# Low pieces of x on GpSimd, and the router's product with its matrix stationary

## The reference, cut to what matters

```python
scores = jax.nn.sigmoid((x @ router_w).astype(jnp.float32))          # 256 x 64
grouped = (scores + router_b).reshape(t, N_GROUPS, N_EXPERTS // N_GROUPS)
group_score = jnp.sum(lax.top_k(grouped, 2)[0], -1)
_, top_groups = lax.top_k(group_score, TOPK_GROUPS)
...
_, idx = lax.top_k(masked, TOP_K)
gate = jnp.take_along_axis(scores, idx, -1)
gate = gate / jnp.sum(gate, -1, keepdims=True) * ROUTED_SCALE
```

## Time and profile before

| | us |
|---|---|
| median of 3 runs | 1355.67 (1354.36 to 1355.84) |
| the profiled execution | 1355.5 |
| its span | 1353.8 |
| PE busy | 1306.0 (96%) |
| DVE busy | 419.1 (31%) |
| ACT busy | 309.5 (23%) |
| POOL busy | 28.2 (2%) |

### The profile page before, as it was taken

The page is one execution under the profiler, slowest core; times in us unless marked ns, Lnnn a source line. Parts: engine busy times, 40 slices in busy tenths (PEclk is TensorE's granted clock), DMA queues, the critical chain, the costliest instruction groups (busy, mean ns, idle before and its releaser), DMA issues.

```text
span 1353.8 us, 16202 instructions
## 1 busy us (share of the span) xinstructions
PE 1306.0 (96%) x6237; PEld 655.2 (48%) x6237; DVE 419.1 (31%) x899; ACT 309.5 (23%) x671; POOL 28.2 (2%) x101
## 2 busy tenths in 40 slices
PE   7999999999999999999979999999999999999996
PEld 5877854344343434444336555444434343443432
DVE  3667364112121121212133655421212212121213
ACT  4354331112111211111121343112111211111112
POOL 1003000000000000000000000000000000000000
PEclk9999989999999999999999998999999999999998
DMA  9315056899999999999992618399999999999992
GB/s 340 127 44 215 1 240 257 324 375 418 418 418 416 417 419 418 417 417 419 418 350 81 248 62 347 150 357 374 418 418 418 416 418 418 418 417 418 418 417 102
DMA packets 93653, 446.27 MB, mean 330 GB/s; under 512 B 9975, under 2 KB 12458, under 8 KB 60330
## 3 DMA queue, kind: packets, MB, share of 16 engines
q1 hardware_dynamic: 93222, 445.51, 81.7%
q10 hardware_dynamic: 388, 0.17, 0.1%
HBM read 444.60 MB, written 1.05 MB: 329 GB/s over the span
## 4 chain that ended last, share of the span: by engine, by line
PE 81%; DMA 12%; DVE 3%; ACT 1%; SPq 1%; issue 1%; DVEq 0%
PE psum L411 28%; PE psum L473 12%; DMA w_up_ring<-in_moe_w_up 12%; PE psum L424 9%; PE psum L465 7%; PE psum L1975 4%; PE psum L2117 4%; PE psum L1095 3%; PE psum L569 2%; PE psum L1538 2%; PE psum L1384 1%; PE psum L1134 1%; PE psum L450 1%; PE psum L602 1%; SPq L294 1%
## 5 line engine op out<-in xcount | busy, mean ns | idle before, releaser
L411 PE MATMUL psum<-w_up_ring,moe_x_selected 128*64 128x512 f32 x2048 | 450.8, 593 | 8.0 <-DMA w_up_ring<-in_moe_w_up 8.0
L411 PEld LDWEIGHTS psum<-w_up_ring,moe_x_selected 128*64 128x64 f32 x2048 | 146.2, 137 | 302.0 <-issue 284.9
L473 PE MATMUL psum<-w_down_ring,moe_hT 128*64 128x512 f32 x992 | 226.5, 598 | 0.9 <-ACT moe_hT L765 0.9
L967 DVE SCALAR_TENSOR_TENSOR moe_h<-moe_silu,moe_slot_gate,psum 128x256 f32<-128x256 f32 x64 | 30.7, 480 | 386.6 <-ACT moe_silu L758 386.6
L473 PEld LDWEIGHTS psum<-w_down_ring,moe_hT 128*64 128x64 f32 x992 | 65.7, 136 | 129.7 <-issue 128.3
L758 ACT ACTIVATE moe_silu<-psum 128x256 f32<-128x256 f32 x64 | 24.7, 385 | 415.2 <-PE psum L411 415.2
L985 DVE TENSOR_TENSOR moe_out_low<-psum,moe_out_high 128x512 fp32r<-128x512 f32 x64 | 44.3, 692 | 233.6 <-ACT moe_out_high L770 233.6
L465 PE MATMUL psum<-moe_out_high,moe_matchT 128*128 128x512 f32 x256 | 113.8, 444 | 0.0
L424 PE MATMUL psum<-moe_match,moe_x_high 128*128 128x448 f32 x256 | 102.4, 400 | 0.0
L465 PE MATMUL psum<-moe_out_low,moe_matchT 128*128 128x512 f32 x256 | 101.4, 396 | 0.0
L424 PE MATMUL psum<-moe_match,moe_x_low 128*128 128x448 f32 x256 | 93.3, 364 | 0.0
(11 more groups left out here) (498 smaller groups left out, 1120.8 us busy)
## 6 DMA issues: line engine op xcount, KB each, us to landing
w_up_ring<-in_moe_w_gate SPq DMA_DIRECT2D x128, 1024.0 KB, 13.1
w_up_ring<-in_moe_w_up SPq DMA_DIRECT2D x128, 1024.0 KB, 15.3
w_down_ring<-in_moe_w_down SPq DMA_DIRECT2D x124, 1024.0 KB, 14.8
w_up_ring<-in_ev_w_in SPq DMA_DIRECT2D x4, 2048.0 KB, 14.2
w_up_ring<-in_od_w_in SPq DMA_DIRECT2D x4, 2048.0 KB, 15.4
w_up_ring<-in_ev_w_out SPq DMA_DIRECT2D x2, 2048.0 KB, 7.8
moe_w_down_extra<-in_moe_w_down SPq DMA_DIRECT2D x4, 1024.0 KB, 16.5
w_up_ring<-in_od_w_out SPq DMA_DIRECT2D x2, 2048.0 KB, 7.7
```

The lines of the kernel that those rows point to most:

```text
L411: last = nc.tensor.matmul(k.psum[e * SLOTS:(e + 1) * SLOTS, 6, :], xsel[:, kk, own:own + SLOTS], up_view(slots[e], kk), start=kk == 0, sto ...
L473: last = nc.tensor.matmul(k.psum[e * SLOTS:(e + 1) * SLOTS, bank, :], hT[:, j * P + e * SLOTS:j * P + (e + 1) * SLOTS], places[e][:, j, ha ...
```

## The change

In each layer: `x_low` is subtracted by POOL, ahead of its memset, and no longer by DVE. The router's product has the router's 128x64 matrix as the stationary operand and 128 tokens as the moving one, so its result is 64 experts by 128 tokens; the sigmoid works on that and writes it to `scores_turned`, and PE turns it back by a transpose into PSUM, which raises `scores`. DVE adds the bias from PSUM, and copies the scores to SBUF with one more operation. ACT takes `scores(0)` ahead of `high_part(0)` and `scores(1)` ahead of `high_part(1)`. On PE, `turn_scores(0)` stands between `turn_x(1)` and `logits(1)`, and `turn_scores(1)` behind the first chunk of `shared_up(0)`.

```diff
+    scoreT = at("scores_turned", [N_EXP, NT, P], F32, end)
...
-                last = nc.tensor.matmul(k.psum[:, 3 * t, 0:N_EXP], k.xT[:, kk, t * P:(t + 1) * P], k.router_w[:, kk, :],
+                last = nc.tensor.matmul(k.psum[0:N_EXP, 3 * t, 0:P], k.router_w[:, kk, :], k.xT[:, kk, t * P:(t + 1) * P],
                                         start=kk == 0, stop=kk == KD - 1)
             last.then_inc(s.logits, 1)
+
+        def turn_scores(t):
+            pe.wait_ge(s.sigmoid, t + 1)
+            nc.tensor.transpose(k.psum[:, 3 * t, P:P + N_EXP], scoreT[:, t, :], k.ident[0:N_EXP, 0:N_EXP]).then_inc(s.scores, 1)
...
         turn_x(1)
+        turn_scores(0)
         logits(1)
         pe.wait_ge(s.shared_w, 32)
-        shared_up(0, range(5))
+        shared_up(0, range(1))
+        turn_scores(1)
+        shared_up(0, range(1, 5))
         pe.wait_ge(s.selected, 1)
...
         def scores(t):
             act.wait_ge(s.logits, t + 1)
-            nc.scalar.activation(score[:, t, :], k.psum[:, 3 * t, 0:N_EXP], ACT.Sigmoid).then_inc(s.scores, 1)
+            nc.scalar.activation(scoreT[:, t, :], k.psum[0:N_EXP, 3 * t, 0:P], ACT.Sigmoid).then_inc(s.sigmoid, 1)
...
         nc.scalar.activation(w1.early[:], w1.ln_eps[:], ACT.Sigmoid)
+        scores(0)
         high_part(0)
         take_xT(1)
-        scores(0)
+        scores(1)
         high_part(1)
-        scores(1)
...
+        for t in range(NT):
+            pool.wait_ge(s.x_high, t + 1)
+            nc.gpsimd.tensor_tensor(x_low[:, t], k.x[:, t, :].rearrange("p (c k) -> p k c", k=KD), x_high[:, t],
+                                    ALU.subtract).then_inc(s.parts, 1)
         pool.wait_ge(s.normed1, NT)
...
         def group_heads(t):
             dve.wait_ge(s.scores, t + 1)
-            step(nc.vector.tensor_tensor(biased[:, t, :], score[:, t, :], k.router_b[:], ALU.add))
+            turned = k.psum[:, 3 * t, P:P + N_EXP]
+            step(nc.vector.tensor_tensor(biased[:, t, :], turned, k.router_b[:], ALU.add))
+            step(nc.vector.tensor_copy(score[:, t, :], turned))
...
         dve.wait_ge(x.router, 32)
-        low_part(0)
         group_heads(0)
-        low_part(1)
         group_heads(1)
```

More of the change, by code:

```diff
@@ L282 @@
     experts="router gu0 gu1 dn0 dn1 dn_extra",
-    moe="mixed variance1 root1 normed1 tables shared_w shared_wd xT_psum xT dve x_high parts logits scores selected places "
+    moe="mixed variance1 root1 normed1 tables shared_w shared_wd xT_psum xT dve x_high parts logits sigmoid scores selected places "
             "table_sb table_dram "
```

## The result

| | us |
|---|---|
| changed kernel, median of 6 runs | 1360.27 (1358.53 to 1361.65) |
| kernel before, the 6 runs timed with it | 1355.76 (1354.36 to 1357.89) |
| ratio, with its 95% interval | 1.0032 (1.0021 to 1.0042) |
| profiled execution of the changed kernel, span | 1359.57, 1357.8 |

The changed kernel is slower by 4.5 us. The forecast was 1364.1, the range 1357.5 to 1367.5. The likeliest case's own range, 1362.5 to 1365.5, was missed.

A forecast was written before the change was run, and what follows sets the result against it. PE was taken to bound the kernel (81% of the chain, DMA 12%). 3.04 + 2.0 + 2 x 1.7 = 8.4 on the profiled 1355.5 gave 1363.9, median 1364.1; 8-in-10 range 1357.5 to 1367.5.

The forecast's parts named there:

- likeliest case: Both layers' routing: POOL holds DVE and PE's clock falls once more per layer; 1362.5 to 1365.5, chance 0.42.
- signs named: Routing: L881 at 1.5 us or more, second subtract 2.4 behind last logits, PE idle before L582, clock fall near gather.
- three signs of being wrong: Routing: L881 keeps 0.19 us while POOL subtracts, the subtract takes under 2 us, or clock stays full through logits(1).
- rival 1: Routing: POOL holds DVE, but the clock doesn't fall again, or in one layer only; 1360.7 to 1362.4, chance 0.25.
- Router's product: PE's 16 router instructions: 0.217 us each, as in the old form; bounds 1.1 us less to 1.0 more per layer.
- rival 3: Before logits(1): denser product keeps the clock from falling, and there is no lock; 4.7 us less, 1351.0, chance 0.06.
- +3.04 and +2.0: Delay in us of PE going on at the counting product (L582), in layer 0 and layer 1, with POOL holding DVE.
- POOL's subtract: low_part(1) on POOL, length T of 2.8 us (bounds 2.1 to 3.8), locks out DVE's two-SBUF-operand operations, first L881.
- The end of the selection without POOL in view: Selection on DVE without the lock: 1.1 us later in layer 0, 0.2 in layer 1, together 1.3.
- PE's clock again: Near the gather: one more clock fall per layer behind PE's still stand, costing 1.7 us each (1.5 to 2.6).
- The delay reaches the end in full: Gather in each layer: every microsecond it starts later moves every refill by a microsecond, counted in full once per layer.
- What was hidden: Routing: low_part(0) on POOL beside one-operand DVE work, later memset and silu table load all stay hidden, no cost added.

The follow-up runs named there:

- e3: Changed kernel with ACT taking high_part(1) ahead of scores(1) again, as before the change; 1353.87 us, ratio 0.9999.
- e8: Changed kernel with seven chunks of shared_up(0) ahead of PE's wait for the selection and one behind, instead of five and three; 1357.78 us, ratio 1.0009.
- e1: Kernel before with the low pieces subtracted by POOL alone; product, sigmoid and ACT's order as before; 1356.02 us, ratio 1.0007.
- e4: Changed kernel without its new product: low pieces on POOL and ACT's new order, old product and sigmoid, nothing turned back; 1359.86 us, ratio 1.0036.
- e6: Changed kernel with POOL's subtract cut into four pieces of 128x256 for each tile; 1359.39 us, ratio 1.0024.
- e7: Changed kernel with one wait more: POOL's second subtract waits for the selection; 1354.41 us, ratio 0.9987.
- e5: Kernel of e3 with seven chunks of shared_up(0) ahead of PE's wait for the selection and one behind, instead of five and three; 1350.69 us, ratio 0.9960.
- e10: Kernel of e5 with the low pieces back on DVE (e2 with the same edit of PE's list); 1353.82 us, ratio 0.9986.
- e2: Changed kernel with low pieces back on DVE and ACT taking high_part(1) ahead of scores(1), so the router's part alone; 1355.72 us, ratio 1.0006.
- e9: Kernel before with PE's filling alone: seven chunks of shared_up(0) ahead of the wait for the selection and one behind; 1355.15 us, ratio 1.0001.

## Why the prediction was right, and where its steps were not

The direction, the range and the cause were right: a subtract on POOL locks out DVE's operations with two SBUF operands, and L887 is held until it ends (so in the changed kernel, e3 and e8; e1, e4, e6 and e7 show the operation that met POOL in its place). The size was nearly twice what was measured: 8.4 against 4.5. Of the signs named, the held operation, the subtract's start, PE's idle time and the fall near the gather were all seen. But one of the three signs of being wrong came true as well: the clock stayed full through `logits(1)`. So the mechanism of the loss was right, and the clock's state before it was not. The time came out 0.4 us under rival 1's range (1360.7 to 1362.4), but rival 1's mechanism, no second fall or only one, is not what the trace shows: the clock fell in both layers.

- **Router's product.** "I take 0.217 for the new form as well": this step failed. The price was read at the half clock, and I assumed that clock for the new kernel. The denser product kept it full: 1.96 us instead of 3.67, so all that stands behind `logits(1)` came 1.7 us earlier in each layer. The bounds, 1.1 us less to 1.0 more, did not hold it. It stood in rival 3 with a chance of 0.06, as a case without the lock. Rival 3 even says what the two together would give, POOL's end setting the selection "at about 206.4 in layer 0" (measured: 206.46), but gives that case no time and no chance; it is what happened. The selection's +3.04 and +2.0 became +1.12 and +0.12, a difference of 3.8, as large as the miss (1364.1 against 1360.3). The clock is 3.4 of it. The rest is the chain behind POOL's end (below) and what the sum gave to the starts of `logits(1)`, 0.12 and 0.1, which the table's distances leave out.
- **POOL's subtract.** T was taken as 2.8 and measured as 2.85. POOL started 2.32 us behind the end of `logits(1)` in layer 0 (200.18 against 197.86); I had 2.32 too (202.05 against 199.73). From POOL's end to the counting product it was 3.43 (206.46 - 203.03), where I added 3.57. The 0.17 us that the sigmoid is said to delay `high_part(1)` stands in no row; the trace after has 0.18 (197.89 to 198.07). The rule itself was stated too narrowly, as e4's L883 shows; in the changed kernel that did no harm, since L887 came first.
- **The end of the selection without POOL in view.** DVE's bias add for tile 1 began at 199.59 and not at 201.7. `turn_scores(1)` started 1.05 us behind the chunk in front of it (197.79 to 198.84), where 1.7 was taken for that chunk, for the same reason of the clock. The copy of the scores cost 0.26 (199.85 to 200.11), as taken (0.22).
- **PE's clock again.** Right: one fall in each layer behind the still stand, 1.64 and 1.71 in "up" against the taken 1.7. That it is no certainty e3 and e6 show, where one layer of two had it; that the price is not fixed, e6's 3.0.
- **The delay reaches the end in full.** Right: +4.59 in the two stretches, +4.5 in the time. Of the ten experiments, seven agree within 1 us between "up" and the medians' distance (e5: -4.29 and -5.2; e10: -3.01 and -2.3). Those that do not are e2 and e3, whose runs divide in two groups, and e9 (+1.21 and -0.9).
- **What was hidden.** `low_part(0)` on POOL, the memset and the silu table load cost nothing here. That `low_part(0)` is harmless depended on the bias add's operand in PSUM; the prediction says only that DVE has one-operand work then, and e1 shows what the add costs with both operands in SBUF.

## What to carry to other kernels

Before work goes to GpSimd, ask what VectorE does during each of its instructions: here a 2.85 us subtract held a 0.19 us operation until it ended, and cutting it up did not help, while moving it 1.8 us earlier or an operand to PSUM did. When a product changes its form, don't carry over a duration taken at the half clock; ask first which clock it will have. And once the selection is early, fill the engine that waits for it: the order of PE's list won nothing before the change (e9) and 3.6 us of the two routing stretches after it (e3 against e5), of which 1.7 is the fall in one layer of e3's trace.

## What the runs showed of the hardware

- POOL's whole 128x1024 subtract with one strided operand took 2.84 or 2.85 us, and 2.89 where it started while DVE's L881 still ran (e4, layer 1), 2.24 times the dense 128x512 one of the earlier trace rows. The strided read that cost DVE a factor of 1.5 (2.03 against two times 0.68) cost POOL at most about 0.3 us.
- Beside POOL's subtract DVE was held in operations with two inputs in SBUF (L887, 0.19 to 2.28) and in a TENSOR_SCALAR with one (e4, L883, 0.17 to 2.38). It was not held in the bias add with one input in PSUM (0.22), in the MAX8 (0.65 for eight) or in a TENSOR_REDUCE with one input (0.28).
- The same router product takes 1.96 us in the new form and 2.00 in the old (`logits(0)` of the kernel before) at full clock; the form matters by the clock behind it, full in 16 of 16 and half in 8 of 8 layers around a still stand of 1.6 us.
- Around PE's later still stands the fall came not every time: with 3.71 us (twice) in the changed kernel, 2.52 (twice) in e2, 2.21 in layer 0 of e4, 2.00 and 1.99 in e8 it came; with 3.35 and 3.34 in e6 and 1.91 (twice) in e3 once each; with 1.62 and 1.25 in e7 and under 1 us in e1, e5, e10 and layer 1 of e4 never. In e2 and e3 the group of runs with the longer times has the lower mean granted clock (0.990 to 0.992 against 0.992 to 0.994). That is part of the spread, not all: e7 and e10, with no fall in their traces, still spread by 3.9 and 3.5 us, and the kernel before by 5.5.
- In layer 0 DVE took up the turned scores 0.48 us behind the end of the transpose (199.11 to 199.59), in layer 1 0.11 behind it. What held it stays open.
